# Gate and up weights of an expert stored with eight neighbouring rows on a partition

## The chip, the cores and the metric

The kernel runs on one core of a Trainium2 chip. The metric is the device time of one execution in microseconds; the lower it is, the better.

## What is computed

One layer of a decoder for 2048 prompt tokens and 32 sample tokens: two mixers, a routed mixture of experts, and a final norm. The change is in the experts alone. Each token goes to two of 32 experts:

```python
def one_group(args):
    xg, e = args                       # 128 rows of 1024, one expert
    return (jax.nn.silu(xg @ w_gate[e]) * (xg @ w_up[e])) @ w_down[e]
```

`w_gate[e]` and `w_up[e]` are 1024 x 256 in fp32, `w_down[e]` is 256 x 1024. The sum over the 1024 input columns can be taken in any grouping into eight lots of 128, as long as the rows of the weights and the columns of the tokens are grouped alike.

## The kernel before, in words

Two sweeps over the 16 tiles of tokens (and the sample rows) come first: the mixers, then the gates, the output projection and the routing. Then the experts: the rows that an expert is to see are listed in blocks of 128 (44 blocks here, and a last one, the "quad", in which four experts have 32 rows each). Two more blocks are worked on ahead, at the end of the second sweep, by `turn_ahead` and `gate_up_of_ahead`. A last stage adds the two results of each token and norms them.

For a block b the engines do this:
- GpSimd gathers 128 rows of 1024 into `gathered` (`xg`), one row on each partition.
- TensorE turns them (`turn`, L2830): eight transposes of 128 x 128, of columns 0 to 127, 128 to 255 and so on. In the profile the block of `gathered` is what is loaded into the array (LDWEIGHTS) and the identity is what streams through (MATMUL). The quad's turn is L2880, that of the two blocks ahead L1611.
- ScalarE and VectorE take the turned block out of PSUM as a high and a low part (`gathered_T_hi` L2575, `gathered_T_lo` L2719).
- ScalarE and VectorE split the expert's gate and up weights, 128 x 4096, into a high and a low part, in two halves of 2048 columns (`gate_up_hi` L2588, `gate_up_lo` L2728; L2620 and L2760 for the first block).
- TensorE multiplies (`gate_up`, through `three`, L168 to L170): for each of eight k, three matmuls of 128 x 512 (256 gate columns and 256 up columns side by side).
- Then silu, a turn of the hidden block (L2853), the down projection (L168 to L170, and L2865), the weighting, and a scatter.

TensorE's order is written out by hand in `step`: gate_up(b), turn(b + 1), out(b - 1), turn_h(b). ScalarE and VectorE have a `step` of their own with the splits of blocks b + 1 and b + 2. The gate and up weights lie in a ring of four slots (`expert_gate_up`, GU = 4096 columns each). SyncE loads a slot with two DMAs of 1 MB (`load_gate_up`, L2155 and L2156) once the slot's last split is done. There are 33 such loads in all.

In a slot, before the change, partition p holds for each k row 128k + p: 256 gate values, then 256 up values. In DRAM each row of `w_gate` is 1 KB, so a partition's share is eight pieces of 1 KB that lie 128 KB apart.

Of the kernel before, what the change touches and what calls it, by code (L numbers as in the profile page):

```python
# [7 lines left out]
F32 = mybir.dt.float32  # L8
# [3 lines left out]
ALU = mybir.AluOpType  # L12
# [3 lines left out]
P = 128  # L16
D = 1024
KD = D // P
# [15 lines left out]
EH = 256  # L34
# [11 lines left out]
RING = 4  # L46
# [1281 lines left out]
def gate_b(nc, a, s, kept, sem, ps, weights, shared, small, ready, early, ahead, load_ahead):  # L1328

    with ExitStack() as ctx:  # L1330
# [67 lines left out]
        took, fullest, cells, records, rows = kept["ahead"]  # L1398
# [6 lines left out]
        a_rows, a_rows_T = (ma, pb), [ahead_T[:, n, :] for n in range(AHEAD)]  # L1405
        a_result = (ma[:, :], a_rows_T[0])
        a_th, a_hidden, a_hidden_T = [xo[:, n * EH:(n + 1) * EH] for n in range(3)]
        a_bank = (3, 1)
        late_out, late_rows_T = 0, 6
        a_weight = lambda n: records[:, n, 2:3].bitcast(F32)  # L1410
        gate_up_ahead = lambda k: ahead["ring"][:, 3 * GU + k * 2 * EH:3 * GU + (k + 1) * 2 * EH]
        down_ahead = lambda k, n: ahead_down[:, k * D + n * 512:k * D + (n + 1) * 512]
        assert AHEAD == 2
        ahead.update(down=ahead_down, selected=(ah_vector, SELECTED), w_in=a_weights, turned=(ah_tensor, TURNED[1]), rows_masked=(ah_vector, ROWS), out_done=(ah_tensor, OUT[1]), stored=a_stored, passed=passed)
# [191 lines left out]
        def turn_ahead(pe, n):  # L1606

            pe.wait_ge(rows_in, 16 * AHEAD)
            pe.wait_ge(h2T_ready, NT + n)
            for k in range(KD):  # L1610
                last = nc.tensor.transpose(ps[late_rows_T + k // 4][:, (k % 4) * P:(k % 4 + 1) * P], a_rows[n][:, k * P:(k + 1) * P], kept["ident"][:, :])  # L1611
            last.then_inc(ah_tensor, 1)

        def gate_up_of_ahead(pe, n, ks):

            pe.wait_ge(a_weights, 48)
            pe.wait_ge(ah_scalar, ROWS_T[n])
            pe.wait_ge(x1_step, NT + 1)
            for k in ks:
                last = nc.tensor.matmul(ps[a_bank[n]][:, :], a_rows_T[n][:, k * P:(k + 1) * P], gate_up_ahead(k),  # L1620
                                        start=(k == 0), stop=(k == KD - 1))
            if KD - 1 in ks:
                last.then_inc(ah_tensor, 1)
# [338 lines left out]
        def on_tensor(pe):  # L1962
# [164 lines left out]
            out(NT, ks=range(7, KD))  # L2127
            route(NT - 1, P)
            turn_ahead(pe, 0)
            join(NT - 1, P)  # L2130
            gate_up_of_ahead(pe, 0, range(0, 4))
# [3 lines left out]
            route(NT, P)  # L2135
            join(NT, P)
            turn_ahead(pe, 1)
            gate_up_of_ahead(pe, 0, range(5, KD))
            rank(NT, P)
            gate_up_of_ahead(pe, 1, range(0, 4))  # L2140
# [6 lines left out]
GU = KD * 2 * EH  # L2147
# [2 lines left out]

def load_gate_up(sp, a, ring, e, slot, done):

    ww = ring[:, slot * GU:(slot + 1) * GU].rearrange("p (k c) -> p k c", k=KD)
    one = lambda t: t[0, bass.ds(e, 1), :, :].rearrange("o (k p) h -> p (o k) h", p=P)
    sp.dma_start(ww[:, :, 0:EH], one(a["w_gate"])).then_inc(done, 16)  # L2155
    sp.dma_start(ww[:, :, EH:], one(a["w_up"])).then_inc(done, 16)  # L2156


def load_down(sp, a, ring, e, slot, done):
# [164 lines left out]
def experts(nc, a, s, kept, sb, sem, ps, ring, downs, listing, ready, outs, ahead):  # L2324

    lists, count_cells = listing
    first_rows = kept["ahead"][2][:, 4:4 + FIXED]
    HG = GU // 2
    xg = sb("gathered", [P, 2, D])
    with nc.sbuf_tensor("quad_T", [P, KD, P], F32) as quad_T:  # L2330
        pass
# [1 line left out]
    wg = ready["split_weights"]  # L2333
    th = sb("tanh_e", [P, EH])
    h = sb("hidden", [P, EH])
# [11 lines left out]
    w_hi, w_lo = sem("e_w_hi"), sem("e_w_lo")  # L2347
# [12 lines left out]
    sumsq, mean, root, done = ready["sumsq"], ready["mean"], ready["root"], sem("c_done")  # L2360
# [4 lines left out]
    t, minus_half = ready["rms"], kept["half"]  # L2365
# [16 lines left out]
    def listed(eng, field, b):  # L2382

        if field == TOTAL:
            return eng.value_load(count_cells[:, 0:1], min_val=NE - QUAD, max_val=MAX_BLOCKS)
        if field == REST:
            return eng.value_load(count_cells[:, 1:2], min_val=(NE - QUAD) // 2 - 2, max_val=PAIRS - 2)
        if isinstance(b, int) and b < FIXED:
            if field == 2:
                return eng.value_load(first_rows[0:1, b:b + 1], min_val=0, max_val=TABLE - P)  # L2390
            return (b, b + 1)[field]
        at = field * P + b
        ap = lists[0:1, at:at + 1] if isinstance(at, int) else lists[0:1, bass.ds(at, 1)]
        return eng.value_load(ap, min_val=(0, 1, 0)[field], max_val=(RING - 1, NE, TABLE - P)[field])
# [165 lines left out]
    def on_scalar(act):  # L2560
# [19 lines left out]
        def weights(b, par, parts=(0, 1)):  # L2580
            slot = listed(act, 0, b)
            if 0 in parts:
                need = listed(act, 1, b)
                act.wait_ge(w_ready, need)
                if not isinstance(b, int) or b > 1:
                    act.wait_ge(gu, b - 1)
            for n in parts:
                nc.scalar.copy(wg[par][0][:, n * HG:(n + 1) * HG], ring[:, bass.ds(slot * GU + n * HG, HG)]).then_inc(w_hi, 1)  # L2588

        def silu(b, par):  # L2590
            act.wait_ge(gu, b + 1)
# [25 lines left out]
        act.wait_ge(ready["o_done"], NT + 1)  # L2617
        act.wait_ge(w_ready, 1)
        for n in range(2):
            nc.scalar.copy(wg[0][0][:, n * HG:(n + 1) * HG], ring[:, n * HG:(n + 1) * HG]).then_inc(w_hi, 1)  # L2620
        ahead["hidden"](act, 0)
        act.wait_ge(ready["scattered"], 32 * (NT + 1))
        act.wait_ge(*ahead["rows_masked"])
# [69 lines left out]
        for n in range(2):  # L2693
            last = nc.scalar.activation(y[:, 0, n * 512:(n + 1) * 512], ps[5 + n][:, :], ACT.Copy, scale=quad_rows[:, 2:3].bitcast(F32))
# [20 lines left out]
    def on_vector(dve):  # L2715
        def turned(b, par):
            dve.wait_ge(xT_hi, b + 1)
            for n in range(2):
                last = nc.vector.tensor_tensor(xT[par][1][:, 4 * n:4 * n + 4, :], ps[n][:, :].rearrange("p (k m) -> p k m", m=P),  # L2719
                                               xT[par][0][:, 4 * n:4 * n + 4, :].bitcast(F32), ALU.subtract)  # L2720
            last.then_inc(xT_lo, 1)

        def weights(b, par, parts=(0, 1)):
            slot = listed(dve, 0, b)
            for n in parts:
                at = slice(n * HG, (n + 1) * HG)
                dve.wait_ge(w_hi, b * 2 + 1 + n)
                nc.vector.tensor_tensor(wg[par][1][:, at], ring[:, bass.ds(slot * GU + n * HG, HG)], wg[par][0][:, at].bitcast(F32),  # L2728
                                        ALU.subtract).then_inc(w_lo, 1)

        def silu(b, par):
# [23 lines left out]

        dve.wait_ge(x_in[0], 16)
        for n in range(2):
            at = slice(n * HG, (n + 1) * HG)
            dve.wait_ge(w_hi, 1 + n)
            nc.vector.tensor_tensor(wg[0][1][:, at], ring[:, at], wg[0][0][:, at].bitcast(F32), ALU.subtract).then_inc(w_lo, 1)  # L2760
            if n == 0:
                turned(0, 0)
        weights(1, 1)
# [58 lines left out]
    def on_tensor(pe):  # L2822
        ident = kept["ident"]

        def turn(b, par, n):
            pe.wait_ge(x_in[par], n * 16 + 16)
            if not isinstance(b, int) or b > 0:
                pe.wait_ge(xT_lo, b)
            for k in range(KD):
                last = nc.tensor.transpose(ps[k // 4][:, (k % 4) * P:(k % 4 + 1) * P], xg[:, par, k * P:(k + 1) * P], ident[:, :])  # L2830
            last.then_inc(x_turned, 1)

        def gate_up(b, par, ks=range(KD)):
# [40 lines left out]
        quarter_rows = lambda c: slice(c * (P // QUAD), (c + 1) * (P // QUAD))  # L2874

        def turn_quad(fore):
            pe.wait_ge(q_x_in, 16)
            pe.wait_ge(xT_lo, fore * 2 + 4)
            for k in range(KD):
                last = nc.tensor.transpose(ps[k // 4][:, (k % 4) * P:(k % 4 + 1) * P], xg[:, 0, k * P:(k + 1) * P], ident[:, :])  # L2880
            last.then_inc(q_tensor, 1)

        def gate_up_quad():
            pe.wait_ge(q_scalar, Q_T)
            pe.wait_ge(q_vector, Q_T_REST)
            pe.wait_ge(w_ready, NE)
            for k in range(KD):
                for c in range(QUAD):
                    at = c * GU + k * 2 * EH
                    last = nc.tensor.matmul(ps[2][quarter_rows(c), :], quad_T[:, k, quarter_rows(c)], ring[:, at:at + 2 * EH],  # L2890
                                            start=(k == 0), stop=(k == KD - 1), tile_position=(0, c * (P // QUAD)))
            last.then_inc(q_tensor, 1)

# [86 lines left out]
def finish(nc, a, s, kept, outs):  # L2980

    with ExitStack() as ctx:
# [22 lines left out]
        with ExitStack() as gates:  # L3005
            gates.enter_context(nc.sbuf_tensor("place_of_gates", [P, 4 * KD * D + 2 * KD * MS], F32))
            raws, split, sample_T, _ = kept["gates"]
            weights = (lambda part, k: split[k // KD][part][:, k % KD, :], lambda k: raws[k // KD][:, k % KD, :],
                       kept["raw_in"], sem("g_raw_hi"), sem("g_raw_lo"), kept["raw_used"],
                       sample_T,  # L3010
                       lambda rows: rows[NT * P:NT * P + MS, :].rearrange("r (j c) -> (r j) c", j=4))
            shared = {}
            g = gate_a(nc, a, s, kept, sem, ps, weights, shared)
            b = gate_b(nc, a, s, kept, sem, ps, weights, shared, small, ready, early, ahead, load_ahead)
# [67 lines left out]
```

## Time and profile before

| | |
|---|---|
| median of 3 runs | 1899.2 us (1898.6 to 1899.38) |
| the profiled execution | 1899.67 us, of which the span is 1898.0 us |
| TensorE busy in the span | 1830.8 us (96%) |
| VectorE, ScalarE, GpSimd busy | 1137.9, 727.8, 229.4 us |
| granted TensorE clock, mean | 0.98 of full |
| expert stage | from about 1362 to about 1825 us |

Busy time is no measure of the bound by itself: matmuls are pipelined, and a matmul's shown duration is longer than its distance to the next. What counts is the chain that ended last, and where TensorE waits.

### The profile page before, as it was taken

The numbers are of one execution on the slowest core, as the hardware profiler recorded it, in microseconds if no ns is written. First come the engines' busy times: TensorE is split into PE (matmuls) and PEld (weight loads), VectorE is DVE, ScalarE is ACT, GpSimd is POOL, SyncE is SP. The second block draws the span as 40 slices with busy tenths as digits, with TensorE's granted clock in tenths as the row PEclk, the third lists the DMA queues.
The fourth block names the chain that finished last, engine by engine and source line by source line (L and its number), as shares of the span: only waits on it lengthen the run. The fifth ranks groups of instructions, "written<-read, shape, count | busy, mean of one in ns | idle before, by whom it ended". The sixth has DMA issues, their size and how long they took to land.

```text
span 1898.0 us, 29695 instructions
## 1 busy us (share of the span) xinstructions
PE 1830.8 (96%) x9077; PEld 1381.1 (73%) x9078; DVE 1137.9 (60%) x2171; ACT 727.8 (38%) x1356; POOL 229.4 (12%) x331
## 2 busy tenths in 40 slices
PE   5999999999999999999899999999899999999987
PEld 2787778777567777777588888888477777777632
DVE  3788888888540000001655555556778888888648
ACT  3444444434330000002321221221477777777522
POOL 0100000000000000000101111101322222222111
PEclk7999999999899999999999999999999999999998
DMA  9322212222485444455844344444889869999587
GB/s 373 108 95 112 108 70 106 112 97 91 181 271 192 177 177 177 177 188 185 307 161 151 133 155 144 155 147 166 273 281 354 292 213 337 328 355 313 193 334 316
DMA packets 175851, 384.40 MB, mean 203 GB/s; under 512 B 30184, under 2 KB 104056, under 8 KB 168572
## 3 DMA queue, kind: packets, MB, share of 16 engines
q1 hardware_dynamic: 139836, 321.28, 47.8%
q0 software_dynamic: 19744, 53.89, 7.6%
q10 hardware_dynamic: 16224, 8.65, 1.5%
q8 instruction: 25, 0.41, 0.1%
q14 instruction: 22, 0.18, 0.0%
HBM read 296.80 MB, written 103.73 MB: 211 GB/s over the span
## 4 chain that ended last, share of the span: by engine, by line
PE 66%; DVE 3%; DMA 2%; issue 1%; ACT 1%; ACTq 0%; POOL 0%; DVEq 0%; SPq 0%; POOLq 0%
PE bank L168 18%; PE bank L170 17%; PE bank L169 17%; PE bank L2865 4%; PE bank L2830 2%; PE bank L2008 2%; PE bank L2970 1%; DMA mixer_parts<-oT_split 1%; PE bank L1307 1%; PE bank L2068 1%; DVE late_x L2807 1%; PE bank L2853 1%; DVE expert_down L2802 0%; DMA gathered<-weighted_rows 0%; DMA expert_down<-weighted_rows 0%
## 5 line engine op out<-in xcount | busy, mean ns | idle before, releaser
L168 PE MATMUL bank<-w_mix_hi,hT_hi 128*128 128x512 f32 (+3 forms) x544 | 203.2, 374 | 3.8 <-DVE hT_lo L610 2.5
L1216 DVE SCALAR_TENSOR_TENSOR ma_rows<-tanh_rows,bank 128x512 f32<-128x512 f32 x32 | 20.6, 684 | 310.2 <-PE bank L170 159.9
L2728 DVE TENSOR_TENSOR gate_up_lo<-expert_gate_up,gate_up_hi 128x2048 fp32r<-128x2048 f32 x86 | 196.4, 2288 | 10.9 <-ACT gate_up_hi L2588 9.9
L169 PE MATMUL bank<-w_mix_hi,hT_lo 128*128 128x512 f32 (+3 forms) x544 | 198.8, 365 | 0.0
L170 PE MATMUL bank<-w_mix_lo,hT_hi 128*128 128x512 f32 (+3 forms) x544 | 198.3, 365 | 0.0
L2588 ACT CAST gate_up_hi<-expert_gate_up 128x2048 fp32r (+1 forms) x86 | 165.1, 1923 | 69.0 <-issue 67.2
L168 PE MATMUL bank<-gate_up_hi,gathered_T_hi 128*128 128x512 f32 x352 | 142.5, 405 | 4.9 <-DVE gathered_T_lo L2719 2.1
L170 PE MATMUL bank<-gate_up_lo,gathered_T_hi 128*128 128x512 f32 x352 | 138.4, 393 | 0.0
L169 PE MATMUL bank<-gate_up_hi,gathered_T_lo 128*128 128x512 f32 x352 | 137.9, 392 | 0.0
L168 PEld LDWEIGHTS bank<-w_mix_hi,hT_hi 128*128 128x128 f32 (+1 forms) x544 | 100.6, 185 | 37.0 <-issue 20.3
L170 PEld LDWEIGHTS bank<-w_mix_lo,hT_hi 128*128 128x128 f32 (+1 forms) x544 | 100.6, 185 | 19.1
L169 PEld LDWEIGHTS bank<-w_mix_hi,hT_lo 128*128 128x128 f32 (+1 forms) x544 | 100.8, 185 | 16.4
L168 PE MATMUL bank<-w_gate_hi,h_parts_b 128*128 128x512 f32 x256 | 103.1, 403 | 6.2 <-issue 5.3
L168 PE MATMUL bank<-w_out_hi,mixer_parts 128*128 128x512 f32 x256 | 100.8, 394 | 1.8 <-DMA mixer_parts<-oT_split 1.8
L168 PE MATMUL bank<-w_gate_hi,h_parts 128*128 128x512 f32 x256 | 102.1, 399 | 0.0
L168 PE MATMUL bank<-w_out_hi,merged_T_hi 128*128 128x512 f32 x254 | 100.4, 395 | 0.6 <-issue 0.6
L170 PE MATMUL bank<-w_gate_lo,h_parts_b 128*128 128x512 f32 x256 | 100.7, 393 | 0.0
L169 PE MATMUL bank<-w_gate_hi,h_parts_b 128*128 128x512 f32 x256 | 100.6, 393 | 0.0
L170 PE MATMUL bank<-w_out_lo,mixer_parts 128*128 128x512 f32 x256 | 100.2, 391 | 0.0
L169 PE MATMUL bank<-w_gate_hi,h_parts 128*128 128x512 f32 x256 | 100.1, 391 | 0.0
L169 PE MATMUL bank<-w_out_hi,mixer_parts 128*128 128x512 f32 x256 | 100.0, 391 | 0.0
L170 PE MATMUL bank<-w_gate_lo,h_parts 128*128 128x512 f32 x256 | 99.9, 390 | 0.0
(463 smaller groups left out, 3833.9 us busy)
## 6 DMA issues: line engine op xcount, KB each, us to landing
expert_gate_up<-in_w_gate SPq DMA_DIRECT2D x33, 1024.0 KB, 9.6
expert_gate_up<-in_w_up SPq DMA_DIRECT2D x33, 1024.0 KB, 13.1
expert_down<-in_w_down SPq DMA_DIRECT2D x32, 1024.0 KB, 12.7
h_parts<-hT_split SPq DMA_DIRECT2D x16, 1024.0 KB, 5.1
mixer_parts<-oT_split SPq DMA_DIRECT2D x32, 512.0 KB, 8.2
w_ada_part<-in_w_ada SPq DMA_DIRECT2D x16, 1024.0 KB, 10.7
h_parts_b<-hT_split SPq DMA_DIRECT2D x16, 1024.0 KB, 4.9
expert_down<-weighted_rows SPq DMA_DIRECT2D x12, 1024.0 KB, 8.2
```

The source lines that it names most:

```text
L168: nc_mm(out, left[0], right[0], start=first, stop=False)
L169: nc_mm(out, left[1], right[0], start=False, stop=False)
L170: return nc_mm(out, left[0], right[1], start=False, stop=last)
L1216: last = nc.vector.scalar_tensor_tensor(out=ma[:, par, at], in0=tg[:, at], scalar=1.0, in1=ps[2 + n][:, :], op0=ALU.add, op1=ALU.mult)
L1307: done = nc.tensor.matmul(ps[6 + half][32 * j:32 * j + R, :], c_now[half][:, :], wc[half][:, j, :], start=first, stop=last, tile_position= ...
L2008: last = nc.tensor.transpose(ps[bank + k // 4][:, (k % 4) * P:(k % 4 + 1) * P], src[:, k * P:(k + 1) * P], ident[:, :])
L2068: last = nc.tensor.matmul(ps[5][rows, 0:m], wr[:, j * KD // 2 + k, :], h2T[:, at], start=(k == 0), stop=(k == KD // 2 - 1), tile_position= ...
L2588: nc.scalar.copy(wg[par][0][:, n * HG:(n + 1) * HG], ring[:, bass.ds(slot * GU + n * HG, HG)]).then_inc(w_hi, 1)
L2728: nc.vector.tensor_tensor(wg[par][1][:, at], ring[:, bass.ds(slot * GU + n * HG, HG)], wg[par][0][:, at].bitcast(F32), ALU.subtract).then_ ...
L2807: nc.vector.tensor_tensor(xc(i, m), xc(i, m), pair[k][0:m, 0, :], ALU.add).then_inc(summed, 1)
L2830: last = nc.tensor.transpose(ps[k // 4][:, (k % 4) * P:(k % 4 + 1) * P], xg[:, par, k * P:(k + 1) * P], ident[:, :])
L2865: last = nc.tensor.matmul(ps[5 + n][:, :], hT_rest[:, :], downs[:, bass.ds(slot * DOWN + D + n * 512, 512)], start=False, stop=True)
```

## The change

The layout of a slot changes. Partition p now holds rows 8p to 8p + 7 of `w_gate` in its first 2048 columns and the same rows of `w_up` in the other 2048. These rows are neighbours in DRAM, so each partition's share of a DMA is one piece of 8 KB. Bytes, number of DMAs and their order stay as they were.

Three things follow from it:
- Step k of the sum now uses rows k, 8 + k, 16 + k and so on. So a turn must take every eighth column of the gathered rows (`eighth_columns`): the 128 values that are loaded into the array from each partition lie 32 bytes apart, where they were neighbours.
- The splits read the slot as 2 x 4 x 256 (two matrices, four k, 256 columns) and write the split weights in the old order (k, then gate and up). So the 24 matmuls of a block read what they read before.
- The quad and the blocks ahead read the ring itself; their moving operand is now two runs of 256 columns, where it was one run of 512.

No instruction is added, removed or moved on any engine or queue; only operands' shapes and strides differ.

```diff
@@ def sweep b, blocks ahead @@
-        gate_up_ahead = lambda k: ahead["ring"][:, 3 * GU + k * 2 * EH:3 * GU + (k + 1) * 2 * EH]
+        gate_up_ahead = lambda k: both_matrices(ahead["ring"][:, 3 * GU:4 * GU], k)
...
-                last = nc.tensor.transpose(ps[late_rows_T + k // 4][:, (k % 4) * P:(k % 4 + 1) * P], a_rows[n][:, k * P:(k + 1) * P], kept["ident"][:, :])
+                last = nc.tensor.transpose(ps[late_rows_T + k // 4][:, (k % 4) * P:(k % 4 + 1) * P], eighth_columns(a_rows[n][:, :], k), kept["ident"][:, :])
...
-                last = nc.tensor.matmul(ps[a_bank[n]][:, :], a_rows_T[n][:, k * P:(k + 1) * P], gate_up_ahead(k),
+                last = nc.tensor.matmul(ps[a_bank[n]][:, :].rearrange("p (g h) -> p g h", g=2), a_rows_T[n][:, k * P:(k + 1) * P], gate_up_ahead(k),
@@ def load_gate_up @@
-    ww = ring[:, slot * GU:(slot + 1) * GU].rearrange("p (k c) -> p k c", k=KD)
-    one = lambda t: t[0, bass.ds(e, 1), :, :].rearrange("o (k p) h -> p (o k) h", p=P)
-    sp.dma_start(ww[:, :, 0:EH], one(a["w_gate"])).then_inc(done, 16)
-    sp.dma_start(ww[:, :, EH:], one(a["w_up"])).then_inc(done, 16)
+    ww = ring[:, slot * GU:(slot + 1) * GU].rearrange("p (g k h) -> p g k h", g=2, k=KD)
+    one = lambda t: t[0, bass.ds(e, 1), :, :].rearrange("o (p k) h -> p (o k) h", p=P)
+    sp.dma_start(ww[:, 0, :, :], one(a["w_gate"])).then_inc(done, 16)
+    sp.dma_start(ww[:, 1, :, :], one(a["w_up"])).then_inc(done, 16)
+
+
+def eighth_columns(rows, k):
+
+    return rows.rearrange("m (q k) -> m k q", k=KD)[:, k, :]
+
+
+def both_matrices(slot, k):
+
+    return slot.rearrange("p (g k h) -> p g k h", g=2, k=KD)[:, :, k, :]
@@ def experts @@
-    HG = GU // 2
+    ring_halves = ring[:, :].rearrange("p (s n c) -> p s n c", s=2 * RING, n=2)
+    loaded_half = lambda slot, n: ring_halves[:, bass.ds(slot * 2, 2), n, :].rearrange("p g (k h) -> p g k h", h=EH)
+    split_half = lambda part, n: part[:, :].rearrange("p (k g h) -> p g k h", g=2, h=EH)[:, :, n * KD // 2:(n + 1) * KD // 2, :]
...
-                nc.scalar.copy(wg[par][0][:, n * HG:(n + 1) * HG], ring[:, bass.ds(slot * GU + n * HG, HG)]).then_inc(w_hi, 1)
+                nc.scalar.copy(split_half(wg[par][0], n), loaded_half(slot, n)).then_inc(w_hi, 1)
...
-                nc.vector.tensor_tensor(wg[par][1][:, at], ring[:, bass.ds(slot * GU + n * HG, HG)], wg[par][0][:, at].bitcast(F32),
+                nc.vector.tensor_tensor(split_half(wg[par][1], n), loaded_half(slot, n), split_half(wg[par][0], n).bitcast(F32),
                                         ALU.subtract).then_inc(w_lo, 1)
...
-                last = nc.tensor.transpose(ps[k // 4][:, (k % 4) * P:(k % 4 + 1) * P], xg[:, par, k * P:(k + 1) * P], ident[:, :])
+                last = nc.tensor.transpose(ps[k // 4][:, (k % 4) * P:(k % 4 + 1) * P], eighth_columns(xg[:, par, :], k), ident[:, :])
...
-                    at = c * GU + k * 2 * EH
-                    last = nc.tensor.matmul(ps[2][quarter_rows(c), :], quad_T[:, k, quarter_rows(c)], ring[:, at:at + 2 * EH],
+                    last = nc.tensor.matmul(ps[2][quarter_rows(c), :].rearrange("p (g h) -> p g h", g=2), quad_T[:, k, quarter_rows(c)],
+                                            both_matrices(ring[:, c * GU:(c + 1) * GU], k),
                                             start=(k == 0), stop=(k == KD - 1), tile_position=(0, c * (P // QUAD)))
```

## Rows read from the trace of the kernel before

**Rows 1.** The page: TensorE's share, DMA busy tenths in 40 slices, packets by size.

```profile
PE 1830.8 (96%) x9077; PEld 1381.1 (73%) x9078; DVE 1137.9 (60%) x2171; ACT 727.8 (38%) x1356; POOL 229.4 (12%) x331
...
DMA  9322212222485444455844344444889869999587
...
DMA packets 175851, 384.40 MB, mean 203 GB/s; under 512 B 30184, under 2 KB 104056, under 8 KB 168572
```

**Rows 2.** Windows: a stretch of the second sweep, and the loop over blocks.

```profile
core 0: us, PE busy (x) PEld busy (x) DVE busy (x) ACT busy (x) POOL busy (x), PEclk, DMA share, GB/s
620.00:900.00 280.00, 280.00 (x1269) 220.45 (x1268) 24.26 (x46) 30.36 (x53) 13.29 (x25) 1.00 0.50 182
1386.00:1773.00 387.00, 386.73 (x1754) 294.58 (x1755) 319.02 (x320) 300.80 (x400) 95.04 (x80) 1.00 0.88 299
```

**Rows 3.** What TensorE waited for from 1364 to 1828 us: total, times, longest.

```profile
PE bank L2916 <- DMA weighted_rows<-y_block,quad_records: 6.0, 1, 6.0
PE bank L168 <- DVE gathered_T_lo L2719: 2.1, 2, 1.2
PE bank L168 <- DVE gate_up_lo L2728: 1.9, 1, 1.9
PE bank L2853 <- DVE hidden L2736: 1.6, 1, 1.6
...
PE bank L168 <- issue: 1.0, 1, 1.0
```

**Rows 4.** The chain that ended last, three blocks: start us, us, what.

```profile
1498.74 0.87 PE bank L2830 x8
...
1508.44 0.87 PE bank L2830 x8
1509.32 0.23 PE bank L168
...
1518.15 0.87 PE bank L2830 x8
```

**Rows 5.** Timeline, 475.3 to 476.4 us: the sample rows' turn, matmuls, then loads.

```profile
475.50 0.68 PE L867 MATMUL bank<-identity,x_rows 32*128 32x32 f32 x8
```

```profile
475.50 0.57 PEld L867 LDWEIGHTS bank<-identity,x_rows 32*128 32x128 f32 x8
```

**Rows 6.** Weight loads of turns grouped by form: count, busy us, mean ns.

```profile
L2830 PEld LDWEIGHTS bank<-identity,gathered 128*128 128x128 f32 x352 | 41.0, 140 | 6.2 <-issue 0.5
...
L1611 PEld LDWEIGHTS bank<-identity,ma_b 128*128 128x128 f32 x8 | 0.9, 140 | 0.2 <-issue 0.2
...
L867 PEld LDWEIGHTS bank<-identity,x_rows 32*128 32x128 f32 x8 | 0.6, 137 | 0.1
...
L867 PEld LDWEIGHTS bank<-identity,w_s_sample_rows 32*32 32x32 f32 x4 | 0.2, 92 | 0.2 <-issue 0.2
```

**Rows 7.** VectorE's and ScalarE's operations grouped by form.

```profile
L2728 DVE TENSOR_TENSOR gate_up_lo<-expert_gate_up,gate_up_hi 128x2048 fp32r<-128x2048 f32 x86 | 196.4, 2288 | 10.9 <-ACT gate_up_hi L2588 9.9 <-issue 0.4
...
L743 DVE TENSOR_TENSOR probs_T<-bank,masks 128x512 f32<-128x512 f32 x32 | 21.7, 679 | 0.0
```

```profile
L2588 ACT CAST gate_up_hi<-expert_gate_up 128x2048 fp32r x80 | 153.9, 1923 | 69.0 <-issue 67.2 <-SPq L2405 1.9
```

**Rows 8.** DMA issues: count, size, median us from issue to landing.

```profile
expert_gate_up<-in_w_gate SPq DMA_DIRECT2D x33, 1024.0 KB, 9.6
expert_gate_up<-in_w_up SPq DMA_DIRECT2D x33, 1024.0 KB, 13.1
...
h_parts<-hT_split SPq DMA_DIRECT2D x16, 1024.0 KB, 5.1
```

**Rows 9.** ScalarE from 1364 to 1828 us: its one wait for a weight load.

```profile
ACT gate_up_hi L2588 <- SPq L2405: 1.9, 1, 1.9
```

**Rows 10.** Timeline of ScalarE at the loop's entry.

```profile
1383.49 0.38 ACT L2592 ACTIVATE tanh_e<-bank 128x256 f32<-128x256 f32 x1 [2.61 <-issue]
```

More of the change, by code:

```diff
@@ L2619, in on_scalar @@
         for n in range(2):
-            nc.scalar.copy(wg[0][0][:, n * HG:(n + 1) * HG], ring[:, n * HG:(n + 1) * HG]).then_inc(w_hi, 1)
+            nc.scalar.copy(split_half(wg[0][0], n), loaded_half(0, n)).then_inc(w_hi, 1)
         ahead["hidden"](act, 0)
@@ L2725, in weights @@
             for n in parts:
-                at = slice(n * HG, (n + 1) * HG)
                 dve.wait_ge(w_hi, b * 2 + 1 + n)
-                nc.vector.tensor_tensor(wg[par][1][:, at], ring[:, bass.ds(slot * GU + n * HG, HG)], wg[par][0][:, at].bitcast(F32),
+                nc.vector.tensor_tensor(split_half(wg[par][1], n), loaded_half(slot, n), split_half(wg[par][0], n).bitcast(F32),
                                         ALU.subtract).then_inc(w_lo, 1)
@@ L2757, in on_vector @@
         for n in range(2):
-            at = slice(n * HG, (n + 1) * HG)
             dve.wait_ge(w_hi, 1 + n)
-            nc.vector.tensor_tensor(wg[0][1][:, at], ring[:, at], wg[0][0][:, at].bitcast(F32), ALU.subtract).then_inc(w_lo, 1)
+            nc.vector.tensor_tensor(split_half(wg[0][1], n), loaded_half(0, n), split_half(wg[0][0], n).bitcast(F32), ALU.subtract).then_inc(w_lo, 1)
             if n == 0:
@@ L2879, in turn_quad @@
             for k in range(KD):
-                last = nc.tensor.transpose(ps[k // 4][:, (k % 4) * P:(k % 4 + 1) * P], xg[:, 0, k * P:(k + 1) * P], ident[:, :])
+                last = nc.tensor.transpose(ps[k // 4][:, (k % 4) * P:(k % 4 + 1) * P], eighth_columns(xg[:, 0, :], k), ident[:, :])
             last.then_inc(q_tensor, 1)
```

## The prediction

> **What bounds the kernel now.** I read the page first: TensorE is busy for 1830.8 of 1898.0 us [rows 1]. That is an average, so I went to the windows of the stage that the change touches. In the loop over blocks, from 1386 to 1773 us, TensorE is busy for 386.73 of 387.00 us at a granted clock of 1.00; VectorE is busy for 319.02 and ScalarE for 300.80 [rows 2]. So there TensorE alone sets the pace, VectorE has 18% to spare and ScalarE 22%. The table of TensorE's waits says the same: between 1364 and 1828 us no wait is for a load of gate or up weights [rows 3]. The chain that ended last runs through TensorE, and shows the period: the turn of a block (L2830) starts at 1498.74, 1508.44 and 1518.15, so a block takes 9.70 us, and the turn has 0.87 us of it [rows 4]. What makes TensorE's stream of a block longer lengthens the kernel, 44 times over. What relieves the DMA engines does not shorten that stream; it could only shorten the few waits at the ends of the loop.
>
> **The DMA's part of the change.** 33 loads of 2 MB go from pieces of 1 KB to pieces of 8 KB: 33 x 2 x 1024 = 67,584 packets become 8,448, most of the 104,056 packets under 2 KB [rows 1]. The DMA engines are busy 0.88 of the loop at 299 GB/s, which is 340 GB/s for a full share; in the sweep whose loads come in 8 KB rows it is 182 at 0.50, so 364 [rows 2]. The mixture will thus get cheaper by some 5 to 10%. Gate and up loads land a median of 9.6 and 13.1 us after their issue, 8 KB rows in the quieter sweep in 5.1 [rows 8]. What would that be worth? ScalarE waited for a weight load once, 1.9 us [rows 9], with a spare 22%, and TensorE not at all for it [rows 3]. I take 0 us for this part. The cover is the ring of four slots; without it the price would be a landing, some 10 us, for each expert.
>
> **The splits.** L2588 and L2728 now read and write runs of 256 columns and more, not one run of 2048. A VectorE operation over 4 runs of 128 columns takes 679 ns for 512 columns, and L2728 2288 ns for 2048 [rows 7]: (2288 - 679) / 1536 = 1.05 ns a column, and 679 - 512 x 1.05 = 141 ns is what is left for the fixed part. So runs of 128 hardly cost anything; I take 0. From above: VectorE's 18% of 9.70 us is 1.7 us a block, and two L2728 of 2288 ns may become 37% longer before TensorE waits. ScalarE has more room. The quad and the blocks ahead stream two runs of 256 columns instead of one of 512; nothing in the trace prices this, it is two short stretches of the whole, and I take 0.
>
> **The turns.** This is the term that decides. A burst is eight pairs of a weight load and a matmul. A burst has 0.87 us of the chain, so the pairs are 109 ns apart [rows 4]. The two sides of a pair overlap, so the slower one sets this distance. How long does the load take, which is the side that now gets the stride? The sample rows' turn tells it: there the matmul streams only 32 columns, but the load still has 128, and the eight loads start (0.57 - 0.137) / 7 = 62 ns apart [rows 5, 6]. The difference between a load of 128 and of 32 columns gives the same: (137 - 92) / 96 = 0.47 ns a column, 60 ns for 128 [rows 6]. So a packed load needs 60 to 62 ns and hides behind 109 ns of matmul. A strided load may take 1.76 times as long for nothing; beyond that every ns counts 8 times a burst.
>
> How much slower a load is whose values lie 32 bytes apart, no row of this trace shows: all its loads are packed. It can be bounded. From below: no slower, 0 us. From above: not slower than walking all that lies between the values, eight times 62 = 496 ns, so (496 - 109) x 8 = 3.1 us a burst and 46 bursts, 142 us. Between the ends the question is how many neighbours come with one fetch, since that many are thrown away now. Two: 2 x 60 = 120 to 124 ns, 0.1 us a burst, 4 to 6 us in all. Four: a matmul of 512 columns has 0.23 us of the chain [rows 4], so 0.45 ns a column on TensorE's other stream, and four such for each of 128 values are 230 ns; by the 62 ns of a packed load it is 248. I take four, which stands in the middle of the ends (1, 2, 4, 8), and of its two prices the 230 ns, since the 0.47 ns a column of a packed load is nearest to that stream's 0.45.
>
> Then a burst takes 8 x 0.230 = 1.84 us in place of 0.87, so 0.97 us more. Bursts on the chain: 44 in the blocks (x352 loads), the quad's, and two ahead (L1611), 47 in all; one of them, at the loop's entry, is followed by idle time of TensorE (1.6 us for `hidden`, 1.0 us "issue" [rows 3]) whose cause is ScalarE's own delay of 2.61 us [rows 10], and this burst hides there. 46 x 0.97 = 44.6 us. The period of a block would be 9.70 + 0.97 = 10.67 us, and VectorE's and ScalarE's waits for TensorE grow by as much, so nothing new becomes late.
>
> The sum against the profiled execution's own time: 1899.67 + 44.6 = 1944.3 us. That execution lies 0.5 us above the median of 1899.2, so I say 1943.8.
>
> The Trainium skill speaks against this change: the page "SBUF — State Buffer", in the note on cachelines under "Door 1", says that SBUF has lines of 16 bytes, that two or more hits on a line are needed to hide the access, and that fp32 can be stepped by at most four elements for free. No run here shows it yet. The page "Vector Engine (DVE) Microarchitecture Reference", section 5.2, gives 1.73 to 2.5 ns a column on VectorE when each element is a hop; were TensorE's load the same, an estimate from that page is 221 to 320 ns a load, and the sum would be 41 to 78 us more. If instead the packed load's price of 60 to 62 ns [rows 6] held for any stride, the sum would be 0.
>
> **The rivals.**
> - *The load stays hidden (33%).* Either the stride costs nothing, or at most a factor of two. For it speaks the room of 1.76 measured above. Then the time is 1899 us, with factor two 1899.2 + 46 x 0.12 = 1905. The change then does what it says to the DMA engines, and nothing comes of it, since TensorE never waits for those loads.
> - *Faster (8%).* Fewer packets free the DMA engines, and what waits at the ends of the loop gets shorter: the 1.6 and 1.0 us at the entry [rows 3], if ScalarE's delay of 2.61 us [rows 10], which comes right behind its issue of small DMAs, is a matter of full queues; and the 1.9 us at the exit. That is at most 1.6 + 1.0 + 1.9 = 4.5 us: 1894.7 us. It decides only if the turns cost less than those 4.5 us, so a load below 109 + 4500 / 46 / 8 = 121 ns. Against it: at the exit TensorE's wait is for VectorE, and no row names a DMA.
> - *Between (10%).* A load of 125 to 195 ns: 46 x 8 x (16 to 86 ns) = 6 to 32 us, so 1905 to 1931 us.
> - *The whole gap is walked (7%).* 496 ns a load: 1899 + 142 = 2041 us.
> - *Likeliest (42%).* A load of 195 to 340 ns. Its own range is 1899.2 + 46 x 8 x (0.086 to 0.231) = 1931 to 1984 us.
>
> **How the numbers follow.** A measurement of this kernel tells about 0.2%, 3.8 us, from no change. Slower: 42 + 10 + 7, and 6 of the hidden case's 33 (a factor just above 1.9), so 65%. Same: the other 27. Faster: 8. The predicted time is that of the likeliest case, 1943.8. The range runs from the hidden case's low end, 1897, to the likeliest's high end, 1985; outside lie the walked gap (7) and most of the faster case, together under 2 in 10.
>
> **What would show it.** In the profile after, each step has its row: the turns' bursts in the timeline (matmuls 230 ns apart), the turn in the chain at 1.84 us, and the period of a block at 10.67 us. The splits should stay at about 1.92 and 2.29 us; the matmuls of gate and up 0.23 us apart. The DMA share in the loop should fall from 0.88, to about 0.75 if the loop also becomes longer. I am wrong if the turns keep their 0.87 us (the hidden case), or if the splits grow beyond 37% and VectorE, not TensorE, sets the period: that would show as waits of L168 for `gate_up_lo` in every block.

## The result and the profile after

The changed kernel takes 1906.28 us (median of 7 runs, 1903.59 to 1907.52), the kernel before 1899.2 us beside it (7 runs, 1895.89 to 1903.02): a ratio of 1.0036, with a 95% interval of 1.0024 to 1.0048. It is slower by some 7 us, where 44.6 were forecast. Measured once more later, it came to 1.0034 (1.0021 to 1.0048).

The page of the changed kernel has the line of the packets, against [rows 1], and the chain that ended last, where a new name stands fourth:

```profile
DMA packets 116715, 384.40 MB, mean 202 GB/s; under 512 B 30184, under 2 KB 36472, under 8 KB 100988
...
PE bank L168 16%; PE bank L170 16%; PE bank L169 16%; DMA gathered<-h_rows,row_tokens 3%; PE bank L2875 3%; PE bank L2840 2%; PE bank L2008 1%; DMA mixer_parts<-oT_split 1%; PE bank L1307 1%; PE bank L2068 1%; DVE late_x L2817 1%; DVE late_x L2821 1%; DVE expert_down L2812 1%; PE bank L2980 1%; ACTq L2406 1%
```

The window of the loop, against [rows 2]; the share is down from 0.88, and TensorE is no longer busy throughout:

```profile
core 0: us, PE busy (x) PEld busy (x) DVE busy (x) ACT busy (x) POOL busy (x), PEclk, DMA share, GB/s
1386.00:1773.00 387.00, 383.25 (x1712) 290.40 (x1711) 311.04 (x313) 295.94 (x390) 92.99 (x78) 1.00 0.80 297
```

The turn is line L2840 now. Two turns in a row from the chain, against [rows 4]:

```profile
1504.52 0.89 PE bank L2840 x8
...
1514.24 0.89 PE bank L2840 x8
```

A burst takes 0.89 us in place of 0.87, and the period is 9.72 us in place of 9.70. 1.84 and 10.67 us were forecast. The groups by form, against [rows 6] and [rows 7], show each strided load longer, 192 ns in place of 140, and the splits unchanged:

```profile
L2840 PEld LDWEIGHTS bank<-identity,gathered 128*128 128x128 f32 x352 | 45.2, 192 | 10.4 <-DMA gathered<-h_rows,row_tokens 7.3 <-issue 0.5
...
L2739 DVE TENSOR_TENSOR gate_up_lo<-expert_gate_up,gate_up_hi 128x2048 fp32r<-128x2048 f32 x86 | 196.5, 2287 | 3.7 <-ACT gate_up_hi L2600 2.1
```

These 192 ns are the busy time of one load and overlap the next: the pairs are 0.89 / 8 = 111 ns apart. The first line also holds what is new. TensorE's loads of the turn stood idle for 7.3 us because the gathered rows were not there. The instructions on `gathered` in the loop, and what they waited for:

```profile
its engine sat idle before it (us, times) until:
  issue: 12.9, 39
  DMA gathered<-h_rows,row_tokens: 9.7, 16
who waited for it (us, times):
  ACT gathered_T_hi L2587: 25.0, 39
  PEld bank L2840: 7.3, 11
  PE bank L2840: 2.4, 5
```

The loads of gate and up weights themselves land sooner than in [rows 8]:

```profile
expert_gate_up<-in_w_gate SPq DMA_DIRECT2D x33, 1024.0 KB, 6.7
expert_gate_up<-in_w_up SPq DMA_DIRECT2D x33, 1024.0 KB, 9.8
```

Two pieces of the chain show one late block; the gather started at 1621.71, took 10.93 us, and the turn began 0.04 us behind it:

```profile
1621.71 10.93 DMA gathered<-h_rows,row_tokens
...
1632.69 1.16 PE bank L2840 x8
```

In the kernel before, a gather of this loop lands after 4.4 to 8.8 us, with a median of 7.7:

```profile
DMA to landing us min/median/max: 4.4/7.7/8.8
```

How much time it has shows GpSimd's timeline of the kernel before. The gather of 1614.72 fills the buffer for the turn that starts at 1624.76, 10.04 us later, and it stands directly behind a scatter that waits for `y_block`:

```profile
1613.15 1.27 POOL L2509 DMA_INDIRECT weighted_rows<-y_block,row_records  x1 [7.20 <-ACT y_block L2614]
1614.72 1.08 POOL L2503 DMA_INDIRECT gathered<-h_rows,row_tokens  x1 [0.30 <-issue]
```

So the kernel before had 10.04 - 8.8 = 1.2 us left at its slowest gather, and the changed one overruns this: its loads wait 11 times and its matmuls 5 times.

### The profile page after: what moved, and what is told of

It is laid out like the page before. It is cut to its first block, busy times and chain, and to the rows that moved or that the text cites. A ratio compares the mean times of both kernels' runs of the same rounds, so it can differ in the third digit from the quotient of the medians.

```text
span 1905.7 us, 29695 instructions
## 1 busy us (share of the span) xinstructions
PE 1832.9 (96%) x9077; PEld 1383.7 (73%) x9078; DVE 1136.2 (60%) x2171; ACT 729.5 (38%) x1356; POOL 229.0 (12%) x331
## 2 busy tenths in 40 slices
DMA packets 116715, 384.40 MB, mean 202 GB/s; under 512 B 30184, under 2 KB 36472, under 8 KB 100988
## 4 chain that ended last, share of the span: by engine, by line
PE 58%; DMA 6%; DVE 5%; issue 2%; ACTq 1%; ACT 1%; POOL 0%; POOLq 0%; DVEq 0%; SPq 0%
PE bank L168 16%; PE bank L170 16%; PE bank L169 16%; DMA gathered<-h_rows,row_tokens 3%; PE bank L2875 3%; PE bank L2840 2%; PE bank L2008 1%; DMA mixer_parts<-oT_split 1%; PE bank L1307 1%; PE bank L2068 1%; DVE late_x L2817 1%; DVE late_x L2821 1%; DVE expert_down L2812 1%; PE bank L2980 1%; ACTq L2406 1%
## 5 line engine op out<-in xcount | busy, mean ns | idle before, releaser
L2739 DVE TENSOR_TENSOR gate_up_lo<-expert_gate_up,gate_up_hi 128x2048 fp32r<-128x2048 f32 x86 | 196.5, 2287 | 3.7 <-ACT gate_up_hi L2600 2.1
L2600 ACT CAST gate_up_hi<-expert_gate_up 128x2048 fp32r (+1 forms) x86 | 165.1, 1922 | 60.8 <-issue 59.3
```

The costliest lines, as they stand in the source:

```text
L2600: nc.scalar.copy(split_half(wg[par][0], n), loaded_half(slot, n)).then_inc(w_hi, 1)
L2739: nc.vector.tensor_tensor(split_half(wg[par][1], n), loaded_half(slot, n), split_half(wg[par][0], n).bitcast(F32), ALU.subtract).then_inc( ...
```

## The experiments

Two theories were to be told apart. **A**: the 8 KB pieces of the weight loads make the gathered rows land late, and the strided turn itself is nearly hidden. **B**: the strided turns cost the whole difference. A third, **C**, was that the order of rows in memory, not the size of a piece, slows the gathers.

The table puts all runs side by side. "39 periods" is the start of the last turn in the loop less that of the fourth turn, from the timelines of the one profiled execution of each kernel; it leaves out the entry and the exit of the loop. "Waits" is the idle time of TensorE's loads and matmuls together until rows had been gathered, from 1386 to 1773 us, each engine's counted for itself, so a late block can count twice; the one wait of gathers_early lies just ahead of that stretch.

| kernel | turns | pieces | gather | ratio to before (95%) | 39 periods, us | waits |
|---|---|---|---|---|---|---|
| before | packed | 1 KB | behind the scatter | 1 | 378.55 | 0 |
| stride_small_pieces | strided | 1 KB | behind | 1.0005 (0.9995 to 1.0015) | 379.32 | 0 |
| pieces_of_4k | strided | 4 KB | behind | 1.0017 (1.0006 to 1.0027) | 381.64 | 2.5, 6 times |
| large_pieces_packed | packed | 8 KB | behind | 1.0055 (1.0037 to 1.0073) | 382.89 | 6.6, 14 times |
| changed kernel | strided | 8 KB | behind | 1.0036 (1.0024 to 1.0048) | 385.92 | 9.7, 16 times |
| changed_again | strided | 8 KB | behind | 1.0034 (1.0021 to 1.0048) | 383.89 | 6.2, 13 times |
| gathers_early | strided | 8 KB | early | 1.0010 (1.0000 to 1.0020) | 379.34 | one, at the entry |
| gathers_early_again | strided | 8 KB | early | 1.0000 (0.9989 to 1.0011) | 379.34 | 0 |
| gathers_early_packed | packed | 8 KB | early | 0.9998 (0.9988 to 1.0008) | 378.54 | 0 |
| gathers_early_before | packed | 1 KB | early | 1.0002 (0.9993 to 1.0011) | 378.54 | 0 |

**The stride without the large pieces.** The rows of an expert lie eight to a partition and the turns are strided, but the slot keeps its old layout:

```diff
     ww = ring[:, slot * GU:(slot + 1) * GU].rearrange("p (k c) -> p k c", k=KD)
-    one = lambda t: t[0, bass.ds(e, 1), :, :].rearrange("o (k p) h -> p (o k) h", p=P)
+    one = lambda t: t[0, bass.ds(e, 1), :, :].rearrange("o (p k) h -> p (o k) h", p=P)
...
-xg[:, par, k * P:(k + 1) * P]
+eighth_columns(xg[:, par, :], k)
```

> Eight neighbouring rows on a partition and the strided turns as in the changed kernel, but the weights still go into the old slot layout, in pieces of 1 KB; the outputs are those of the reference. Theory A (the 8 KB pieces make the gathered rows land late; the strided load itself is nearly hidden): the turn's burst stays at 0.89 us in the chain of waits, no block waits 10 us for its rows, and the time is 0.018 us x 46 = 0.8 us above the kernel before, about 1900. Theory B (the strided turns cost the whole difference, for instance because turns that end later start the next gather later): about +7 us, 1906, with late gathers in half of the blocks as in the changed kernel.

It measured 1.0005, with an interval that holds 0.8 us and leaves out 7, as theory A expects. In its trace 39 periods grow from 378.55 to 379.32 us, 20 ns a block, with no wait for rows. Its first and last turn:

```profile
1387.82 1.05 PE L2835 MATMUL bank<-identity,gathered 128*128 128x128 f32 x8
...
1767.14 1.05 PE L2835 MATMUL bank<-identity,gathered 128*128 128x128 f32 x8
```

Theory B falls. So does C: the rows lie in the new order here, and the gathers land as before:

```profile
DMA to landing us min/median/max: 4.5/7.6/8.8
```

**The large pieces without the stride.** This run computes other gate and up products, as its expectation says.

```diff
-eighth_columns(xg[:, par, :], k)
+xg[:, par, k * P:(k + 1) * P]
```

> The changed kernel with its turns taking 128 neighbouring columns again, as in the kernel before. It changes the computation: the columns of a turned row no longer meet the weight rows that lie on their partition, so the gate and up products are other numbers; instructions, pieces and waits are the same in number and size. Theory A: +5 to +7 us against the kernel before, about 1905, with pieces of the chain of waits of some 10 us on the gathered rows, and the turn's burst back at 0.87 us. Theory B: no more than 1 us above the kernel before.

It measured 1.0055 on 6 runs of its own, about 10 us and so more than theory A's 5 to 7; the interval reaches down to 7 us. Its turns are back at 0.87 us, and the late gathers are there:

```profile
1416.54 9.85 DMA gathered<-h_rows,row_tokens
1474.95 10.82 DMA gathered<-h_rows,row_tokens
1573.33 10.70 DMA gathered<-h_rows,row_tokens
1671.16 10.86 DMA gathered<-h_rows,row_tokens
1700.99 10.51 DMA gathered<-h_rows,row_tokens
```

The 39 periods take 4.3 us more than before. The profiled run took 9.7 us more than the profiled kernel before. Of the rest, 3.1 us lie at the loop's entry, from the third turn to the fourth (15.76 us in place of 12.68), where TensorE ran partly at half clock (below), and 2.0 us ahead of the first turn of all (1363.92 in place of 1361.89). So the ratio of 1.0055 is not all late gathers; its interval and that of the changed kernel overlap.

**Pieces of 4 KB.** Each piece is cut in two, and the slot holds the first four rows of gate and of up, then the last four.

```diff
-    one = lambda t: t[0, bass.ds(e, 1), :, :].rearrange("o (p k) h -> p (o k) h", p=P)
+    one = lambda t: t[0, bass.ds(e, 1), :, :].rearrange("o (p n k) h -> p (o n) (k h)", p=P, n=2)
```

> The changed kernel with each 8 KB piece cut in two of 4 KB (the slot holds the first four weight rows of gate and of up, then the last four), strided turns; the outputs are those of the reference. Theory A: the share of a DMA engine that a gather gets beside a weight load follows the size of the load's pieces, so the gathers are late more seldom: between the kernel before and the changed one, +1 to +4 us. Theory B: +7 us, as the changed kernel, since the turns are the same. A third theory, C, that it is the new order of rows in memory and not the size of a piece that delays the gathers: +7 us here and also with pieces of 1 KB.

It measured 1.0017, 3.2 us, and stands between the two, as A expects. The waits are 6 in place of 16:

```profile
  DMA gathered<-h_rows,row_tokens: 2.5, 6
```

**Gathers issued early.** The kernel has two buffers of gathered rows, and the gather of block b+3 needs nothing but the turn of block b+1. It was still queued behind the scatter of block b-1.

```diff
-        def step(b, slot, landed):
-            gather(b + 2, (slot + 2) % 4, landed)
+        def step(b, slot, landed, more=None):
+            if more is None:
+                gather(b + 3, (slot + 3) % 4, landed)
+            else:
+                with pool.If(more):
+                    gather(b + 3, (slot + 3) % 4, landed)
             scatter(b - 1, (slot - 1) % 4)
...
```

> The changed kernel with GpSimd's queue in another order: in the step of block b it issues the gather of block b+3 ahead of the scatter of block b-1, and no longer the gather of block b+2 behind the scatter of block b-2, so a gather starts as soon as the turn that frees its buffer is over, some 9 us earlier. Theory A: the gathers land well before their turns, the chain of waits shows no piece on the gathered rows, all blocks have the undisturbed period of 9.73 us: the time is that of the kernel before plus 0.8 us for the turns less some 1.6 us at the exit, 1898 to 1900.5. Theory B (late rows are only the sign of something else that delays TensorE): 1904 to 1907, the time goes to another wait.

It measured 1.0010 and, once more, 1.0000. GpSimd's timeline shows the gather ahead of the scatter:

```profile
1607.72 1.02 POOL L2515 DMA_INDIRECT gathered<-h_rows,row_tokens  x1 [2.96 <-issue]
1613.22 1.29 POOL L2521 DMA_INDIRECT weighted_rows<-y_block,row_records  x1 [4.48 <-ACT y_block L2631]
```

The turn that it feeds starts at 1625.08, so it has 17.4 us in place of 10.04. It also lands sooner, though the weight pieces are still of 8 KB: gathers of this loop take at most 8.3 us here and 9.4 in the repeat, where the late ones behind a scatter, in the chains above, took 9.85 to 10.93.

```profile
DMA to landing us min/median/max: 3.2/7.6/8.3
```

```profile
DMA to landing us min/median/max: 3.1/7.7/9.4
```

Both are below the 10.04 us that the gathers had behind the scatter. So the large pieces delay a gather beyond its time only at its old place; whether its standing behind a scatter in the same queue does it, or the moment at which it meets the weight loads, these runs do not separate. Nothing in the loop's chain waits for rows any more, and 39 periods take 379.34 us, the number of the strided turns with small pieces. One wait is left, of 1.0 us for the load and 0.6 for the matmul, ahead of the loop's entry in the first of the two runs.

> The changed kernel with early gathers once more, beside the run without the stride on the same chip: the first measurement was 1.0010 [1.0000, 1.0020] of the kernel before. Theory A expects 0.8 us for the strided turns and nothing else, a ratio of 1.0004; the first measurement, taken at its face, 1.9 us.

The second measurement holds A's 1.0004. The two of them together do not tell 0.8 us from nothing.

**The same order on the kernel before.** The edit is the same.

> The kernel before (weights in 1 KB pieces, packed turns) with GpSimd's queue reordered as in the run with early gathers: the gather of block b+3 ahead of the scatter of block b-1. Theory A: no wait on gathered rows is on the path of the kernel before, so the reorder gives nothing there: within 0.1% of it, 1896 to 1900. Theory B (the reorder is a gain by itself, whatever the pieces): 3 us or more below the kernel before.

It measured 1.0002, and its 39 periods take 378.54 us against 378.55. So the early gather is no gain of its own; it only pays where rows come late.

**Early gathers without the stride.** This run too computes other gate and up products.

> The changed kernel with both of its suspects removed: gathers issued early, and turns of 128 neighbouring columns, which changes the computation (the columns of a turned row no longer meet the weight rows on their partition, so gate and up products are other numbers). What is left of the change is the 8 KB pieces alone. Theory A says that they cost nothing once the gathers are early: within 0.1% of the kernel before, and some 0.8 us below the run with early gathers and strided turns. If the large pieces cost something of their own, beside the late gathers, it shows here as 2 us or more.

It measured 0.9998, and 39 periods take 378.54 us. The 8 KB pieces, once the gathers are out of the way, cost nothing and bring nothing that a measurement with an interval of 0.1% either way can tell. So no version tried here is measurably faster than the kernel before.

**The changed kernel again.**

> The changed kernel once more, so that it has the same chip and the same runs of the kernel before as the next one. Theory A (the 8 KB pieces make gathered rows land late) and the first measurement both say 3 to 5 parts in a thousand above the kernel before, some +6 to +9 us; a result within 1 in a thousand would mean that the first measurement was a matter of the chip.

It measured 1.0034, so the first result stands. How many gathers come late differs between executions of one kernel: 16 waits in the first trace, 13 here.

**The price of a stepped load by itself.** At TensorE's end, on buffers that are free by then:

```diff
+        def stepped(apart):
+            return xg[:, 0, 0:P * apart].rearrange("m (q k) -> m k q", k=apart)[:, 0, :]
+
+        for apart in (1, 2, 4, 8, 1):
+            for k in range(16):
+                nc.tensor.transpose(ps[7][:, 0:P], stepped(apart), ident[:, :])
+        for apart in (1, 2, 4, 8, 1):
+            for k in range(16):
+                nc.tensor.matmul(ps[7][:, 0:16], stepped(apart), ident[:, 0:16], start=True, stop=True)
```

> The kernel before with 160 more transposing matmuls at TensorE's end, into a bank that is free by then; nothing is left out. Their weights are 128 values of each partition of the gathered rows, taken 1, 2, 4, 8 and again 1 values apart, 16 instructions each; first with a moving tile of 128 columns as in the turns, then with one of 16 columns, so that the pace is set by the weight load itself. If the strided load is hidden as the changed kernel's trace says, the first series keeps a pace of 0.11 us at every distance, and the second shows the load's own price: about 60 ns packed, and at 8 apart more than that but at most 111 ns, which is what the turns of the changed kernel took a pair. The term that I had recorded (230 ns) would show 200 ns or more in both series at 8 apart. About 160 x 0.1 = 16 us are added to the time.

The first series at a granted clock of 1.00, by loads: those with values 4 apart, 8 apart, and neighbouring again. Each row is a stretch of 14 loads, 13 steps from the first to the last start:

```profile
L2983 PEld LDWEIGHTS bank<-identity,gathered x14: 208/209/211, 1894.5 to 1896.0; 128*128 128x128 f32 x14
```

```profile
L2983 PEld LDWEIGHTS bank<-identity,gathered x14: 192/193/195, 1896.4 to 1897.8; 128*128 128x128 f32 x14
```

```profile
L2983 PEld LDWEIGHTS bank<-identity,gathered x14: 138/141/143, 1898.2 to 1899.6; 128*128 128x128 f32 x14
```

By the starts themselves, unrounded, the pairs are 120, 112 and 109 ns apart. The second series has moving tiles of 16 columns, and each of its 80 instructions left two loads and two matmuls in the trace. It shows first neighbouring values at a clock of 1.00, 112 ns a load. Then the granted clock fell to 0.50. There, 4 apart, 8 apart and neighbouring:

```profile
L2986 PEld LDWEIGHTS bank<-identity,gathered x30: 328/329/330, 1909.8 to 1916.5; 128*128 128x128 f32 x30
```

```profile
L2986 PEld LDWEIGHTS bank<-identity,gathered x30: 333/336/338, 1917.2 to 1924.1; 128*128 128x128 f32 x30
```

```profile
L2986 PEld LDWEIGHTS bank<-identity,gathered x30: 333/333/338, 1924.8 to 1931.0; 128*128 128x128 f32 x30
```

That is 6.9 / 29 = 238 ns for loads 8 apart and 6.2 / 29 = 214 ns for packed ones: a factor of 1.11. The expectation of 60 ns for the packed load at full clock was missed (112), and so was the cost of the 160 instructions: the one run took some 36 us more and not 16, since the second series is twice as many records and most of all of them ran at half clock. The forecast's 230 ns is not there at full clock: what the turns do is 112 ns. How a load 8 apart runs at full clock with 16 columns this does not show, since the clock fell too soon.

## Why the prediction was wrong

**What bounds the kernel** was right as far as it went. TensorE alone set the pace of the loop. But the prediction had read only the waits that existed, and added "so nothing new becomes late". The deadline of the gathers, 10.04 us against a slowest landing of 8.8, stood in the same trace, and no step looked at it. GpSimd's queue is not in the sum at all.

**The turns** were the step that failed: "I take four ... and of its two prices the 230 ns". The sign of this term held, its size did not. The term of 0.97 us a burst measured 0.02: 39 periods grew by 379.32 - 378.55 = 0.77 us, so 46 bursts cost 0.9 us in place of 44.6. Two assumptions went into it. The first was that neighbours in one fetch are lost; the loads 8 apart take 1.11 times the packed ones at half clock, not four times. The second was that the sample rows' pace of 62 ns is that of any packed load. It is not: with 128 rows and a moving tile of 16 columns the pace is 112 ns. Which of the two differences makes it so, the rows or the form of the matmul, was not tried. The case in which the load stays hidden was a rival at 33%, and for the turns it is what happened. But the room of 1.76, which spoke for it, was not confirmed: with moving tiles of 16 columns in place of 128, though in another form of matmul, the packed pairs are no closer together (112 ns against 109).

The Trainium skill, in "SBUF — State Buffer", says in the note on cachelines under "Door 1" that fp32 can be stepped by at most four elements for free; it gives no price beyond that. For VectorE's or other accesses no run here tests it. For TensorE's weight loads the traces do not agree: a step of four was not free (120 ns a pair against 109), and a step of eight cost less than that, 2 to 3 ns a pair in the turns.

**The DMA's part**, put at 0, is the other step that failed: it had the right rows and the wrong question. The loads did land sooner (6.7 and 9.8 us), the share fell to 0.80, and neither is worth anything, as forecast. But I asked only who waits for these loads, not what shares the engines with them. The gathers do. The term that I left out measured 385.92 - 378.55 - 0.77 = 6.6 us in the profiled execution, 4.6 in that of the repeat, 4.3 with packed turns, and 2.3 with pieces of 4 KB. With early gathers it is 0.

That the large pieces delay the gathers is shown by the runs; how the engines come to do it is read from the traces. Two queues share the engines in the loop. In the kernel before, from 1395 to 1770 us:

```profile
q1 hardware_dynamic: 64622, 86.84, 68.4%
q0 software_dynamic: 11232, 26.68, 19.2%
```

and in the changed one:

```profile
q1 hardware_dynamic: 15462, 86.43, 60.5%
q0 software_dynamic: 10944, 25.72, 18.4%
```

The mean packet of q1 took 0.684 x 16 x 375 / 64622 = 64 ns of an engine before, and 235 ns after; one of q0, which has the gathers and the scatters, 103 and 101 ns. So the gathers' own packets are no slower. If an engine takes a packet from each queue in turn, each of theirs waits behind one that is 3.7 times as long. The profile counts one packet for each piece: the change took away 175,851 - 116,715 = 59,136 packets, and 67,584 - 8,448 pieces are as many. Single microseconds in which the two queues together keep the engines busy show such an alternation; they are picked for that and are no averages, and packets at their edges count whole. The kernel before from 1424.5 to 1425.5 us, with pieces of 1 KB:

```profile
q0 software_dynamic: 81, 0.33, 81.0%
q1 hardware_dynamic: 81, 0.08, 23.1%
```

Pieces of 4 KB, from 1622.5 to 1623.5 us:

```profile
q1 hardware_dynamic: 62, 0.19, 46.7%
q0 software_dynamic: 58, 0.24, 57.8%
```

The changed kernel from 1418 to 1419 us, with pieces of 8 KB:

```profile
q1 hardware_dynamic: 27, 0.20, 56.3%
q0 software_dynamic: 27, 0.11, 32.9%
```

The counts are about one to one in all three, and q0 moves 0.33, 0.24 and 0.11 MB in its microsecond. Sharing by bytes or by time would have left it about the same share of the engines each time, and it has 81, 58 and 33%. In the changed kernel's microsecond from 1428.5 us, one of the highest beside 8 KB pieces, it still has no more than 42% (42 packets to 35). An estimate from these rows: a 1 KB packet takes 0.231 x 16 / 81 = 0.05 us of an engine and one of 8 KB 0.563 x 16 / 27 = 0.33. A gather of 128 rows has 128 / 16 = 8 packets on each engine, if they are spread evenly, so it lasts up to 8 x 0.29 = 2.3 us longer. From a median of 7.7 and a slowest of 8.8 us that leads to 10.0 and 11.1, and the late ones of the chains above took 9.85 to 10.93. The Trainium skill states such an alternation ("DMA: Bandwidth & Descriptors", section "Queues, rings and completion order": an engine goes round-robin between queue rows, a packet at a time), and the counts agree with it. What it calls a packet there is a group of some 9 to 17 descriptors, and whether that is what the profile counts as one these runs do not show; the counts above are the profile's.

**The splits** at 0 were right: 2287 and 1922 ns, as before. So was the 0 for the quad and the blocks ahead: their matmuls over two runs of 256 columns take 594 and 598 ns on average, before and after.

**The faster rival** named 1.9 us at the exit and 1.6 + 1.0 at the entry. The exit did shorten, from 1783.80 - 1770.36 = 13.44 us to 1792.07 - 1780.26 = 11.81, but the change need not have done it: the run of load prices, with 1 KB pieces and packed turns, has 11.77 us there, and the one with large pieces and packed turns 13.39. The waits are the same, 1.9 and 1.8 us. Behind them the matmuls take 0.43 us in the chain of before and 0.23 in that of after:

```profile
1778.41 0.43 PE bank L170
1778.84 0.43 PE bank L168
```

```profile
1788.36 0.23 PE bank L169
1788.60 0.23 PE bank L170
```

**The range** of 1897 to 1985 us holds 1906.28. It leaned on a term that was not there, and that the kernel came out slower at all was luck: most of the 7 us is the gathers', which the prediction had nowhere.

## What to carry to other kernels

When a transfer that nobody waits for is cut into larger pieces, look at the other transfers that run beside it and at how much time each has left before its reader: 1.2 us at the slowest was not enough here. Such a loss was cured here by an earlier issue, without giving the pieces up; the gather was in GpSimd's queue behind a scatter that it had nothing to do with, and ahead of it the same pieces cost nothing. And where no row shows a price, as with the strided load, a middle value picked between ends of 0 and 142 us is no forecast; 160 instructions at the end of the kernel would have priced it beforehand, at 112 ns a pair.

## What the runs showed of the hardware

- A weight load of 128 fp32 values 32 bytes apart takes 192 ns where a packed one takes 140, by the profile, and the pairs of load and transposing matmul move from 109 to 111 ns. A distance of 16 bytes was slower than one of 32 at full clock: 120 ns a pair against 112.
- After one short stop TensorE's clock fell in some executions and not in others. After the 1.9 us wait at the loop's exit, the kernel before ran at a granted clock of 0.72 from 1777 to 1783 us, and the changed kernel, after its wait of 1.8 us, at 1.00 from 1786 to 1792. That the kernel does not decide it, the two runs of early gathers show, which are one kernel: the first has 11.79 us from the last turn of the loop to the next and the second 13.39. So an execution gains or loses 1.6 us there by itself.
- At the entry of the loop the run with large pieces and packed turns had a granted clock of 0.63 from 1388 to 1397 us, where the kernel before had 1.00 from 1386 to 1392. It is no matter of the pieces alone: the run of early gathers on the kernel before, with pieces of 1 KB, had 0.72 from 1386 to 1392. Part of the scatter of single times, 1893 to 1903 us for the kernel before, may be this; it was not tried.
- Beside a queue with 8 KB pieces, a queue with 4 KB packets had 33% of the DMA engines in a microsecond that both filled; beside 1 KB pieces it had 81%. Packets went about one for one, 27 to 27 and 81 to 81.
- In the run of load prices the granted clock went from 1.00 to 0.50 within the stretch from 1903.30 to 1909.45 us, where TensorE was busy throughout with loads and moving tiles of 16 columns.
